# Shift and gate rows by way of DRAM, and router beside sums of squares

## The reference, cut to what matters

```python
mod = silu(c) @ w_ada + b_ada                 # (9, 6 * 1024)
sh1, sc1, gt1, sh2, sc2, gt2 = split(mod, 6)
h = rmsnorm(x, norm1_g) * (1 + sc1) + sh1
x = x + gt1 * token_mixer(h, ...)             # in-projection to 9216, pooling, retention, up, out
h = rmsnorm(x, norm2_g) * (1 + sc2) + sh2
x = x + gt2 * moe(h, ...)                     # router h @ w_router + b, top 4 of 32 experts
y = rmsnorm(x, final_norm_g)
```

## Time and profile before

| what | value |
|---|---|
| median of three timed runs | 1615.55 us |
| the profiled execution, its own time | 1610.57 us |
| its span, first to last instruction | 1608.8 us |
| PE busy | 1480.3 us, 92% |
| DVE, ACT, POOL busy | 308.3, 206.3, 156.4 us |
| mean granted PE clock | 0.957 of full |
| read from HBM, written | 507.6 MB, 30.5 MB |

### The profile page before, as it was taken

How to read it: one execution, slowest core, us unless ns; L and a number is a source line. 1 busy time by engine, 2 the same in 40 slices (tenths; PEclk the granted TensorE clock), 3 DMA queues, 4 the chain that set the end, 5 groups by cost and what they waited for, 6 DMA issues and landing times.

```text
span 1608.8 us, 17919 instructions
## 1 busy us (share of the span) xinstructions
PE 1480.3 (92%) x6906; PEld 733.0 (46%) x6907; DVE 308.3 (19%) x593; ACT 206.3 (13%) x385; POOL 156.4 (10%) x221
## 2 busy tenths in 40 slices
PE   6999999988999899999998998998998998999993
PEld 3777887656877533333333333333333332333331
DVE  1022114324211411212111112112112112112113
ACT  3000213533000210101001000000001000000001
POOL 0230000100620001000000000100000000000000
PEclk9999999999999899999999999999999999999996
DMA  9767634997355465679999999999999999999991
GB/s 363 292 245 279 216 131 175 369 408 275 86 184 210 157 240 214 249 300 426 422 418 422 423 423 424 419 413 426 425 414 421 411 425 417 423 409 422 419 414 57
DMA packets 78617, 533.56 MB, mean 332 GB/s; under 512 B 7561, under 2 KB 8673, under 8 KB 51729
## 3 DMA queue, kind: packets, MB, share of 16 engines
q1 hardware_dynamic: 67330, 503.47, 76.6%
q0 software_dynamic: 10864, 28.72, 5.5%
q10 hardware_dynamic: 391, 0.93, 0.2%
HBM read 507.62 MB, written 30.50 MB: 334 GB/s over the span
## 4 chain that ended last, share of the span: by engine, by line
PE 61%; DMA 33%; DVE 3%; SPq 1%; issue 1%; ACT 1%; DVEq 0%; ACTq 0%; POOL 0%; POOLq 0%
DMA ring<-in_w_expert_in_dram 26%; PE ps L924 15%; PE ps L945 15%; PE ps L748 13%; PE ps L497 3%; DMA vslot<-in_state_ret_dram 3%; DMA out_dram<-vslot 2%; PE ps L841 2%; PE ps L791 2%; DMA ring<-in_w_ada_dram 2%; PE ps L806 2%; PE ps L799 2%; PE ps L888 2%; PE ps L896 1%; PE ps L544 1%; DMA vslot<-in_w_up_ret_dram 1%
## 5 line engine op out<-in xcount | busy, mean ns | idle before, releaser
L924 PE MATMUL ps<-ring,xgT 128*64 128x512 f32 x1632 | 405.4, 642 | 41.9 <-DMA ring<-in_w_expert_in_dram 41.4
L748 PE MATMUL ps<-hT,ring 128*128 128x264 f32 x1152 | 269.6, 392 | 4.5 <-ACT hT L1021 2.3
L924 PEld LDWEIGHTS ps<-ring,xgT 128*64 128x64 f32 x1632 | 120.6, 147 | 303.5 <-issue 248.2
L748 PEld LDWEIGHTS ps<-hT,ring 128*128 128x128 f32 x1152 | 219.2, 192 | 59.5 <-issue 20.0
L945 PE MATMUL ps<-moe_ring,actT 128*64 128x512 f32 x1088 | 242.6, 598 | 0.4 <-ACT actT L1165 0.4
L945 PEld LDWEIGHTS ps<-moe_ring,actT 128*64 128x64 f32 x1088 | 78.0, 137 | 140.4 <-issue 135.6
L1486 DVE COPY xg<-ps 128x512 f32<-128x512 f32 x35 | 24.2, 691 | 610.6 <-PE ps L888 610.6
L924 PE MATMUL ps<-moe_ring,xgT 128*64 128x512 f32 x544 | 122.5, 592 | 0.0
L888 PE MATMUL ps<-rows,picked 128*64 128x512 f32 (+1 forms) x420 | 101.4, 599 | 1.7 <-ACT x_rows L1149 1.7
L1161 ACT ACTIVATE glu_s<-glu_g 128x512 f32<-128x512 f32 x34 | 21.4, 629 | 447.3 <-DVE glu_g L1498 447.3
L924 PEld LDWEIGHTS ps<-moe_ring,xgT 128*64 128x64 f32 x544 | 39.1, 137 | 77.7 <-issue 77.7
(11 more groups left out here) (273 smaller groups left out, 1065.4 us busy)
## 6 DMA issues: line engine op xcount, KB each, us to landing
ring<-in_w_expert_in_dram SPq DMA_DIRECT2D x96, 2048.0 KB, 16.6
moe_ring<-in_w_expert_out_dram SPq DMA_DIRECT2D x64, 2048.0 KB, 10.7
moe_ring<-in_w_expert_in_dram SPq DMA_DIRECT2D x32, 2048.0 KB, 17.8
ring<-in_w_in_dram SPq DMA_DIRECT2D x18, 2048.0 KB, 11.1
ring<-in_w_ada_dram SPq DMA_DIRECT2D x12, 2048.0 KB, 9.3
ring<-in_state_ret_dram SPq DMA_DIRECT2D x8, 1024.0 KB, 11.4
vslot<-in_state_ret_dram SPq DMA_DIRECT2D x8, 1024.0 KB, 12.8
out_dram<-ring POOLq DMA_DIRECT2D x8, 1024.0 KB, 9.2
```

What stands on the lines that cost most here:

```text
L748: mm = nc.tensor.matmul(ps[:, j, 0:T], ring[s][:, k, j * P:(j + 1) * P], hT[:, k, :], start=(k == 0), stop=(k == KC - 1))
L924: mm = nc.tensor.matmul(side(bank, g), xgT[:, 2 * j + a, :], w[:, a, c * COL:(c + 1) * COL], start=False, stop=(j == 3 and a == 1))
```

## The change

- POOL loads b_ada for gt1 to gt2 into b_rows, each 512 columns repeated over 32 partitions (eight DMAs after the constants). stage_rows(1) and (2) add b_rows where they copied; take_columns(1) and (2) then copy where they added.
- POOL stores the rows of sh2 and gt2 out of mod_stage 1 and 2 to kept_rows in DRAM (four DMAs), and loads them back after the in-projection: sh2 of the prompt repeated on 128 partitions as sh_rows, that of the samples as sh_sample, gt2 as gate_rows. DVE waits for the four stores before the state copies that overwrite the buffer, PE for the three loads before the output projection.
- mod_rows_turned, the spreads of shift_rows and sample_spread go, and so do ACT's eight copies. shift_rows goes; g_final has its place.
- The sums of squares of the first norm come after the second w_ada chunk.
- In scaled_turned the sum of squares stands right behind the router matmul, ahead of the transposes.

```diff
+    kept_rows = nc.dram_tensor("kept_rows", (2, NB, D), F32, kind="Internal").ap()
+        b_rows = [at(f"b_rows{b}", [P, COL], misc + 2048 * b) for b in range(2)]
         gate_rows = new("gate_rows", [NB, D])
-        shift_rows = new("shift_rows", [NB, D])
-        g_final = at("g_final", [P, D], top[0] - size([NB, D]))
+        g_final = new("g_final", [P, D])
...
# PE
                     ada_rows(at_load, p)
-                    if p == 0:
+                    if p == 1:
                         pe.wait_ge(vec_copied, 1)
                         sum_squares(0)
-                    elif p == 1:
                         pe.wait_ge(x_copied, KC)
                         old_inputs_turned()
...
-            def mod_rows_turned():
-                for g in range(4):
-                    for k in range(4):
-                        mm = turn(ps[0:NB, 4 + g, k * P:(k + 1) * P], modT[:, (40, 44, 24, 28)[g] + k, :])
-                    mm.then_inc(mod_turned, 1)
...
-            def prompt_spread():
+            def shifts_spread():
                 pe.wait_ge(sw_ready, 1)
-                for h in range(2):
-                    nc.tensor.matmul(ps[:, 5 + h, :], const("selc", NB)[:, 0:P], shift_rows[:, h * COL:(h + 1) * COL],
-                                     start=True, stop=True).then_inc(spread_rows, 1)
                 for t, (t0, n) in enumerate(TILES):
                     mm = nc.tensor.matmul(ps[0:n, 7, t * E:(t + 1) * E], const("selc", NB)[:, t0:t0 + n], sw[:], start=True, stop=True)
                 mm.then_inc(spread_rows, 1)
-            def sample_spread():
...
-            pe.wait_ge(mod_rows, 8)
+            pe.wait_ge(rows_back, 48)
...
             def scaled_turned(k):
                 pe.wait_ge(xs_ready, k + 1)
                 pe.wait_ge(xs_sample, k + 1)
+                pe.wait_ge(sq_ready, KC + k + 1)
                 nc.tensor.matmul(ps[0:E, 6, 0:T], routew[:, k, :], xs[:, k, :], start=(k == 0), stop=(k == KC - 1))
+                nc.tensor.matmul(ps[E:2 * E, 6, 0:T], ones[:, 0:E], sq[:, k % 2, :], start=(k == 0), stop=(k == KC - 1)).then_inc(xs_used, 1)
                 for t in range(2):
                     turn(ps[:, 2 * t + k // 4, (k % 4) * P:(k % 4 + 1) * P], xs[:, k, t * P:(t + 1) * P])
...
-                pe.wait_ge(sq_ready, KC + k + 1)
-                nc.tensor.matmul(ps[E:2 * E, 6, 0:T], ones[:, 0:E], sq[:, k % 2, :], start=(k == 0), stop=(k == KC - 1)).then_inc(xs_used, 1)
# DVE
...
                 dve.wait_ge(ada_ready, ready)
-                cp(mod_stage[b][:], ps[:, 4 + b, :]).then_inc(ada_staged, 1)
+                if b == 0:
+                    cp(mod_stage[b][:], ps[:, 4 + b, :]).then_inc(ada_staged, 1)
+                else:
+                    dve.wait_ge(rows_biased, 16 * 8)
+                    tt(mod_stage[b][:], ps[:, 4 + b, :], b_rows[b - 1][:], ALU.add).then_inc(ada_staged, 1)
...
             take_block(9, 3)
+            dve.wait_ge(rows_kept, 64)
             for h in range(HEADS):
                 take_state(2 * h)
# POOL
...
             pool.dma_start(ct[:, EARLY_W:CONST_W], consts[:, EARLY_W:CONST_W]).then_inc(late_const, 16)
+            for g in range(8):
+                pool.dma_start(b_rows[g // 4][GROUP * (g % 4):GROUP * (g % 4 + 1)],
+                               b_ada[:, 2 * D + g * COL:2 * D + (g + 1) * COL].broadcast_to([GROUP, COL])).then_inc(rows_biased, 16)
...
             pool.dma_start(new_pool_sample[0, :, BUF - 1], u_rows[BUF:BUF + TS]).then_inc(tail_stored, 16)
+            pool.wait_ge(ada_staged, 3)
+            for g in range(4):
+                kind, half = g // 2, g % 2
+                pool.dma_start(kept_rows[kind, :, half * COL:(half + 1) * COL], mod_stage[1 + kind][GROUP * (2 + half):GROUP * (2 + half) + NB]).then_inc(rows_kept, 16)
             pool.wait_ge(tail_stored, 48)
...
+            pool.wait_ge(rows_kept, 64)
+            pool.wait_ge(in_ready, 4 * IN_BLOCKS)
+            pool.dma_start(sh_rows[:], kept_rows[0, 0:1].broadcast_to([P, D])).then_inc(rows_back, 16)
+            pool.dma_start(sh_sample[:], kept_rows[0, 1:NB]).then_inc(rows_back, 16)
             pool.wait_ge(o_normed, 1)
+            pool.dma_start(gate_rows[:], kept_rows[1]).then_inc(rows_back, 16)
             for i in range(3):
                 pool.dma_start(b_full[32 * i:32 * i + 32], b_expert_in[0]).then_inc(bias_in, 16)
```

More of the change, by code:

```diff
@@ L1121, in _ @@
                         nc.scalar.activation(o_rs[:], o_rs[:], ACT.Sqrt).then_inc(std_ready, 1)
-            for g in range(4):
-                act_e.wait_ge(mod_turned, g + 1)
-                half = slice(g % 2 * COL, (g % 2 + 1) * COL)
-                nc.scalar.copy((gate_rows, shift_rows)[g // 2][:, half], ps[0:NB, 4 + g, :]).then_inc(mod_rows, 1)
-            for h in range(2):
-                act_e.wait_ge(spread_rows, h + 1)
-                nc.scalar.copy(sh_rows[:, h * COL:(h + 1) * COL], ps[:, 5 + h, :]).then_inc(mod_rows, 1)
-            for h in range(2):
-                act_e.wait_ge(spread_rows, h + 4)
-                nc.scalar.copy(sh_sample[:, h * COL:(h + 1) * COL], ps[0:TS, 4 + h, :]).then_inc(mod_rows, 1)
             for k in range(KC):
@@ L1227, in stage_rows @@
                 dve.wait_ge(ada_ready, ready)
-                cp(mod_stage[b][:], ps[:, 4 + b, :]).then_inc(ada_staged, 1)
+                if b == 0:
[3 more added lines that the diff above has]
+                    tt(mod_stage[b][:], ps[:, 4 + b, :], b_rows[b - 1][:], ALU.add).then_inc(ada_staged, 1)
             def take_columns(b):
                 dve.wait_ge(ada_turned, b + 1)
-                tt(modT[:, 16 * b:16 * b + 16, :].rearrange("p (g j) n -> p g j n", j=4),
-                   ps[:, ADA_TURNED[b], :].rearrange("p (j g n) -> p g j n", j=4, g=4)[:, :, :, 0:NB],
-                   vecT[:, 16 * b:16 * b + 16].rearrange("p (g j) -> p g j", j=4).unsqueeze(3).broadcast_to([P, 4, 4, NB]),
-                   ALU.add).then_inc(mod_ready, 1)
+                mod = modT[:, 16 * b:16 * b + 16, :].rearrange("p (g j) n -> p g j n", j=4)
+                turned = ps[:, ADA_TURNED[b], :].rearrange("p (j g n) -> p g j n", j=4, g=4)[:, :, :, 0:NB]
+                if b == 0:
+                    tt(mod, turned, vecT[:, 0:16].rearrange("p (g j) -> p g j", j=4).unsqueeze(3).broadcast_to([P, 4, 4, NB]), ALU.add).then_inc(mod_ready, 1)
+                else:
+                    cp(mod, turned).then_inc(mod_ready, 1)
             stage_rows(0, ADA_FIRST)
@@ L1389, in _ @@
                     step(nc.vector.memset(lt[:], 0.0))
-                    dve.wait_ge(spread_rows, 3)
+                    dve.wait_ge(spread_rows, 1)
                     step(cp(rb[:, 0:2, :], ps[:, 7, 0:2 * E].rearrange("p (t e) -> p t e", t=2)))
```

11 lines of the change are left out of this document (3 added, 8 removed).

## The result

The changed kernel takes 1599.7 us (median of six runs, 1597.37 to 1600.67), where the kernel before took 1614.92 on the same chip (six runs, 1613.95 to 1619.29): ratio 0.9901, 95% interval 0.9888 to 0.9914. That is 15.2 us less, where I forecast 11.65 less and 1603.9. The time lies inside the range (1598.5 to 1610.5), near its lower end, and 0.8 under the narrower range that I had given for the forecast itself (1600.5 to 1607): the change gains more than I had reckoned.

The account below looks back on a forecast made before the run. PE was taken to bound the kernel, its expert stage moving with the stages ahead. Start -0.2, up-projections +8.1 and output projection +3.75 sum to 11.65 us off, giving a median of 1603.9 us, range 1598.5 to 1610.5.

Parts of the forecast that it names:

- What bounds it, and that the expert stage moves with what is ahead: Whole kernel: PE holds 61% of the span, DMA 33%; the unchanged expert stage starts when the stages ahead end.
- Start, -0.2: First adaLN chunks: sums of squares one chunk later finish hT at 34.6, 0.15 past when awaited; 0.2 us lost.
- The bound of 2.1: Start: the most it could lose, in us, if PE did the sums of squares at the slower clock after waiting.
- Bias rows, kept rows, DVE's new wait: Extra loads and stores by POOL, and DVE's wait for four stores near 210 us: all covered, cost 0.
- Rival 3: Near 210 us: DVE's state copies wait for the four stores and the kernel gets slower, 1624 at a 231 us landing; chance 0.04.
- Up-projections, the part on PE, 5.25: Transposes (1.75), two spreads (1.8) and the clock's fall (1.7) go, so vslot's load is issued 5.25 us sooner.
- The load of vslot, 11.5 us in the forecast: Up-projections: issued at 447.3, it escapes the clearing, lands at 458.8 and still ends PE's wait; stage gain 8.1 us.
- the clearing cost it 2.9 us: Up-projections: stores clearing moe_rows took 1.12 MB, or 2.9 us, from vslot's load, which took 14.3 us.
- bound of 8.8: Up-projections: the largest gain in us, if PE alone decides, ready at 458.1 instead of 466.92.
- Output projection, 3.75: Router and squares overlap, 0.6 instead of 1.12 us: 3.0 over six turns, 0.75 from the last two.
- The bound of 4.2: Output projection: the largest gain in us, if the second call of the pair is wholly free.
- The median: Timed runs: the profiled execution lies 5.0 us below their median, so span 1598.9 gives a median of 1603.9.

Follow-up runs that it names:

- before_again: The kernel before, unedited, profiled a second time: 1614.6 us in one run, with 1064.4 us from the turn of lt to the end.
- spread9_four: Changed kernel plus four unused matmuls of 9 rows and 512 columns where the shift-row spreads were: 1610.2 us, one run; up-projections 96.87 us.
- spread9: Changed kernel plus two unused matmuls of 9 rows and 512 columns where the shift-row spreads were: 1599.9 us, one run; up-projections 90.85 us.
- clear_late: Kernel before, with POOL's two clearing stores of moe_rows held until vslot's second load landed: 1608.2 us, ratio 0.9977 to the kernel before.
- same_group: Changed kernel with the router's matmul in the squares' column group, in another bank: 1606.0 us, one run; output stage 41.40 us.
- four_groups: Changed kernel with router and squares of two blocks side by side in four column groups, every second block: 1595.4 us, ratio 0.9885 to the kernel before.

## Why the prediction was right, point by point

- **What bounds it, and that the expert stage moves with what is ahead:** right, though one sign of being wrong occurred. I had asked that the stage from the first expert matmul to the end be 1037.5 long within 3, and it is 1040.5. The bound was too narrow: before_again, the same kernel as before, has 1040.4, and the 14 profiles run from 1037.3 to 1044.9.
- **Start, -0.2:** right in size (0.3 by 14 profiles); the first load's moment, which the sum could not know, outweighed it. The bound of 2.1, beside which I had named the Trainium skill (TensorE: Matmul & The Clock Gate, "HAM oscillation — how this bites in real kernels"), did not occur: PE was idle 1.23 on the second chunk, and the sums behind it took 4.83 as before. The waits in the case that the page describes are longer than that one, so it bore less on this start than I had it.
- **Bias rows, kept rows, DVE's new wait:** priced at nothing, and no wait on them shows. Rival 3 did not occur.
- **Up-projections, the part on PE, 5.25:** 5.16 by the issue of vslot's load (46.52 after the stage's start before, 41.36 after). The fall of the clock went with the spreads, and in spread9_four it came back with four such matmuls. That it would go was right. The reason I gave, the 9 of 128 rows, is not shown: two such matmuls at the same point of the order (spread9) and the kernel's own sample spread were followed by no fall.
- **The load of vslot, 11.5 us in the forecast:** 9.5. The term "the clearing cost it 2.9 us" was too small; clear_late puts it at 4.7. So PE and not the load decides, and 1.05 us more were gained. Of these, 0.7 is the load. The rest is PE, whose bound of 8.8 was too low as well: from the load's issue to the matmuls on it PE took 10.49, not 10.8, and 0.11 less behind them, since a group that waited takes 3.83 and one that follows its neighbour 3.72.
- **Output projection, 3.75:** 5.24, the term most mis-sized. The end, which runs into ACT, gave the 0.75 of the forecast; the six turns ahead of it gave 4.49 and not 3.0. The forecast took 0.5 a turn; it is 0.75, of which same_group gives 0.43 to the overlap, near the forecast, and 0.32 to the order itself. I had set the cost of the other shape between (0.12 a call above its bare columns) against one call. The bound of 4.2 left it out as well. The sentence on the Trainium skill's rule of the drain (TensorEngine Tiling (Array Packing), "Key Properties") pointed to it: same_group agrees with the rule in that two changes of tiling mode (rows times columns of the engine that a matmul uses, `128*32` or `128*128` in the rows) fewer saved 0.32, about 0.1 in each of three places. I had weighed it as part of a call and not beside it, also in the sum by the page's rule, 0.45 more.
- **The median:** I carried the profile's distance of 5.0 under the median over to the new kernel. Its profile lay 0.5 under the median. So 1603.9 is 4.2 too high although the span was met: the three stages gained 3.4 more than their terms, and the kernel before itself came out at 1614.92 instead of 1615.55. What the two profiles differ in is the rest stage, and that hid 3.6 us of gain in the spans.

## What to carry to other kernels

Small matmuls of the same tiling mode want to stand together, in different column groups: the overlap gives one part (0.43 us a turn here), and the mode changes that go with it nearly as much (0.32). A few microseconds of help work on PE in front of a load's issue cost more than their own length, when they delay the load into another queue's transfer. Judge a change of this size by the length of its stages, each from its own profile, since they repeat to 0.1 us, whereas the expert stage behind them wanders by 8.5.

## What the runs showed of the hardware that was not expected

- Four float32 calls with weights of 32 columns, on four column groups, start within 0.02 us of each other and take about as long as one: 0.58 us over 264 tokens in four_groups, where a single call took 0.56 before.
- Two stores of 528 KB each in a second queue lengthened a 2.1 MB load from 9.6 to 14.3 us, where the bytes lost in their 5 us explain 2.9 of the 4.7.
- Two matmuls of 9 rows and 512 columns were followed by a fall of the clock in four profiles of four where the kernel before has its prompt spread, and by none in the same four where it has its sample spread, nor in spread9; four of them were followed by a fall in the one profile that has them. What decides is open.
